# Two MLP boundaries of a three-layer block on one Trainium2 core: the second token tile is normed earlier, GpSimd takes one weight split and one weighting, one square moves between the turned pieces

## The chip, the cores and the metric

One core of a Trainium2 chip runs the whole program: TensorE multiplies, VectorE (DVE in the profile), ScalarE (ACT) and GpSimd (POOL) do the work between the products, and SyncE (SP) issues the loads of the weights. The metric is the device time of one execution in microseconds (us).

## What is computed

Three transformer layers on 512 tokens of width 1024, all in float32. The layers' attention and gating parts don't matter here. What matters is how an MLP ends and what stands behind it:

```
def _rms_norm(x, g):
    y = xf * lax.rsqrt(jnp.mean(xf * xf, axis=-1, keepdims=True) + NORM_EPS)
    return (y * g).astype(x.dtype)

def _squared_relu_mlp(x, w1, w2):
    h = jax.nn.relu(x @ w1)
    return (h * h) @ w2

# layer 0 and layer 1
    f = _squared_relu_mlp(_rms_norm(h, norm_g[layer, 2]), ffn_w1[layer], ffn_w2[layer])
    h = h + _rms_norm(f, norm_g[layer, 3])
# the next part begins with
    xn = _rms_norm(h, norm_g[layer, 0])          # layer 1: the SGU mixer
    h = rms_norm(x, norm_mix[l]) * (1.0 + sc1) + sh1   # third layer: attention
```

So behind each of the two squared-ReLU MLPs a **boundary** follows: square f and weight it with the gain row, add it to h, square h, norm it, turn it (tokens by features to features by tokens), multiply with the next weights. There are two of these boundaries, one behind layer 0 and one behind layer 1.

## The kernel before, in words

**Weights.** All weights pass through two slots `w_raw` of 128x2048. A float32 product is made of three TensorE products of rounded parts: ScalarE writes the rounded part (`split_hi`, L704, `w_hi`), VectorE the rest (`split_lo`, L1347, `w_lo = w_raw - w_hi`), and `mm3` (L2118 to L2120) multiplies hi x hi, hi x lo and lo x hi. SyncE loads tile n as soon as `w_lo_ready` tells that tile n-2 is split.

**Order.** No scheduler: each engine runs one list that is written out by hand, with counting semaphores between them. What stands on an engine behind a waiting instruction waits too.

**A boundary.** Tokens stand in four tiles t of 128 rows; f is in `m` (parts 0 and 1 of the MLP already summed) and in PSUM (the last part). `post` exists once on ScalarE and once on VectorE, with `partial` true at our two boundaries (passes 3 and 7, `p` = 2 and 4). TensorE ends the MLP in `tail`: it finishes the sums of tiles 0, 1, 2, turns tiles 0 and 1 (`transposed`, L2142, 8 transposes each, waits on `xs_ready`, which `normed` of that tile sets), multiplies the last 12 products of tile 3, and then goes into `head`. The head multiplies the first two weight tiles of the next part (`head_hi`, `head_lo`, in places of their own) with tokens 0 to 255 (a = 0), turns tiles 2 and 3, and goes on with tokens 256 to 511 (a = 1). Within the first head tile it waits for each of the eight 128-row pieces of x (`x_ready`).

VectorE's steps in `post` are: `head_split_lo` (L1404: a subtraction of 128x2048 with both inputs in SBUF), `add_sum` (L1463: m + PSUM, 128x1024), `gained` (L1425: m times `row_gain`, both in SBUF), `joined` (L1431: h = m * rstd + h, both in SBUF), `normed` (L1374: h * rstd into m), `turned_lo` (L1396 in the first boundary; L1394, L1390, L1392 in the second, which also adds a bias). ScalarE's are: `head_split_hi` (L801), `sum_square` and `h_square` (L739 with a root, L744; 1024 wide), `turned_hi` (L773; L770, L771, L766 in the second). `rooted` (L1368) is a reciprocal of one column.

**GpSimd** sums the modulation of the third layer in six chunks (`ada_chunk`, L663 tensor_scalar and L664 tensor_tensor of 128x1024, both on SBUF), three of them early in layer 0's MLP and three in layer 1's. Between the halves it masks `w_s` (L675) and makes four small roots, behind them come two iotas. In the boundaries it has nothing but the eight maskings.

Of the kernel before, what the change touches and what calls it, by code (L numbers as in the profile page):

```python
# [20 lines left out]
F32 = mybir.dt.float32  # L21
F32R = mybir.dt.float32r
I32 = mybir.dt.int32
ALU = mybir.AluOpType
# [82 lines left out]
def program(nc, A, out):  # L107

    S, N_TILES, N_UNITS = plan()
# [21 lines left out]
    with ctx:  # L131
# [55 lines left out]
        m = place("m", [P, NT, D], M_)  # L187
# [91 lines left out]
        def sem(name):  # L279
            return ctx.enter_context(nc.semaphore(name))  # L280
# [41 lines left out]
            "h_ready", "gate_used", "y_value", "y_hi_ready", "cmp_loaded", "cmp_x_ready", "cmp_step"))  # L322
        final_done, stored = sem("final_done"), sem("stored")
        tail_gained, tail_rstd = sem("tail_gained"), sem("tail_rstd")

# [50 lines left out]
        def turned_piece(p, a, k):  # L376

            bank_ = 4 * a + (S[HEADS[p]].unit + (0, 1, 0, 1, 2, 3, 2, 3)[k]) % 4
            c = (0, 0, 1, 1, 0, 0, 1, 1)[k] * 256
            return ps[:, bank_, c:c + 256]  # L380
# [218 lines left out]
        def _(pool):  # L599
# [56 lines left out]
            def ada_use(cc, k):  # L656
# [9 lines left out]
                if k == DK - 1:  # L666
                    pool.sem_inc(ada_sum, 1)

            pool.wait_ge(c_ready, 1)
            for cc in range(3):  # L670
                ada_chunk(cc)

            pool.wait_ge(ws_loaded, 16)
# [10 lines left out]
            for cc in range(3, 6):  # L684
                ada_chunk(cc)

            nc.gpsimd.iota(col_no[:, 0:256], pattern=[[1, 256]], base=0, channel_multiplier=0).then_inc(f_made, 1)
# [8 lines left out]
        def _(act):  # L696
# [60 lines left out]

            def turned_hi(p, a):

                for k in range(DK):  # L760
                    src, dst, gain = turned_piece(p, a, k), x_hi[:, k, 256 * a:256 * a + 256], col_gain[:, p, k:k + 1]
                    act.wait_ge(xt_done, x_base(p, a) + (3, 4, 3, 4, 7, 8, 7, 8)[k])
# [18 lines left out]
            def post(pass_no, e, partial, h_before, p):  # L781
# [30 lines left out]
                h_square(1)  # L812
                sum_square(2)
                turned_hi(p, 0)
                sum_square(3)
# [525 lines left out]
        def _(dve):  # L1341
# [76 lines left out]
            def post(pass_no, e, partial, row_no, p):  # L1418
# [23 lines left out]
                joined(1)  # L1442
                normed(0, e + 2)
                if partial:
                    add_sum(pass_no, 2)
                normed(1, e + 3)
                head_split_lo(p, 1)
                turned_lo(p, 0)
                if partial:
                    add_sum(pass_no, 3)  # L1450
                for t in (2, 3):
                    gained(t)
                    joined(t)
                normed(2, e + 6)
# [1494 lines left out]
```

## Time and profile before

| | us |
|---|---|
| median of 3 runs | 2027.57 (2027.54 to 2028.61) |
| the profiled execution | 2027.51 |
| its span | 2025.8 |
| PE busy in the span | 2000.7 (99%) |
| DVE, ACT, POOL busy | 1013.0, 702.0, 340.8 |
| TensorE clock granted | 0.999 |

The span is the part between the first and the last instruction that the profile records; the execution's own time is 1.7 us longer. In the timelines below, the first boundary lies at 640 to 673 us and the second at 1284 to 1318 us. Busy PE says little on its own: what counts is where TensorE stands still, and its idle time is put behind the instruction that ended it.

### The profile page before, as it was taken

The page shows a single profiled execution, that of the slowest core. Times are in us where ns is not written, and L with a number is a line of the kernel's source. Part 1 is how long each engine was busy: PE and PEld are TensorE (multiplying, and loading weights), DVE is VectorE, ACT ScalarE, POOL GpSimd, SP SyncE. Part 2 cuts the span into 40 slices and gives each one's busy share as a digit, 9 for nine tenths or more (in the row PEclk, how much of TensorE's full clock was granted, in tenths as well). Part 3 has the DMA queues.
Part 4 walks back from the last instruction along what each step waited for, and adds up shares of the span by engine and source line. Part 5 has one row for each costly group of instructions (what it writes and reads, how often), then busy time and mean ns, then how long its engine had stood idle before and what let it go on. Part 6 is the DMA issues. An engine that isn't in the chain of part 4 may idle for free.

```text
span 2025.8 us, 26755 instructions
## 1 busy us (share of the span) xinstructions
PE 2000.7 (99%) x10855; PEld 1675.0 (83%) x10855; DVE 1013.0 (50%) x1400; ACT 702.0 (35%) x1012; POOL 340.8 (17%) x199
## 2 busy tenths in 40 slices
PE   9999999999999999999999999999999999999998
PEld 7878888888888888889888888888877788888887
DVE  5358858438255435626735534642443654322345
ACT  6356743232124422315213212533433343212213
POOL 1000006858100001000585720000000200000000
PEclk9999999999999999999999999999999999999999
DMA  6211044544323233132453532222222232332321
GB/s 201 77 49 43 24 133 138 179 130 166 104 95 108 78 104 94 66 111 87 163 187 116 174 112 88 83 84 76 81 64 77 70 104 92 106 104 89 98 104 63
DMA packets 135031, 208.89 MB, mean 103 GB/s; under 512 B 6346, under 2 KB 105864, under 8 KB 134920
## 3 DMA queue, kind: packets, MB, share of 16 engines
q1 hardware_dynamic: 125952, 180.37, 27.5%
q0 software_dynamic: 6912, 25.17, 3.8%
q10 hardware_dynamic: 2056, 1.76, 0.3%
q8 instruction: 84, 1.38, 0.3%
q14 instruction: 27, 0.22, 0.0%
HBM read 205.18 MB, written 2.10 MB: 102 GB/s over the span
## 4 chain that ended last, share of the span: by engine, by line
PE 92%; DVE 4%; ACT 2%; issue 1%; POOL 1%; ACTq 0%; POOLq 0%; DVEq 0%
PE ps L2118 27%; PE ps L2120 27%; PE ps L2119 27%; PE ps L2179 1%; PE ps L2559 1%; PE ps L2570 1%; PE ps L2678 1%; PE ps L2172 1%; PE ps L2171 1%; PE ps L2775 1%; PE ps L2142 1%; POOL gate_t L691 1%; DVE w_lo L1347 0%; ACT w_hi L704 0%; PE ps L2548 0%
## 5 line engine op out<-in xcount | busy, mean ns | idle before, releaser
L1347 DVE TENSOR_TENSOR w_lo<-w_raw,w_hi 128x2048 fp32r<-128x2048 f32 x149 | 347.7, 2334 | 569.5 <-ACT w_hi L704 569.4
L2118 PE MATMUL ps<-x_hi,w_hi 128*128 128x512 f32 x1240 | 489.2, 394 | 1.4 <-ACT v_sw L906 0.8
L2120 PE MATMUL ps<-x_hi,w_lo 128*128 128x512 f32 x1240 | 483.0, 390 | 0.0
L2119 PE MATMUL ps<-x_lo,w_hi 128*128 128x512 f32 x1240 | 482.9, 389 | 0.0
L704 ACT ACTIVATE w_hi<-w_raw 128x2048 fp32r<-128x2048 f32 x151 | 288.9, 1913 | 526.4 <-PE ps L2120 425.4
L2118 PEld LDWEIGHTS ps<-x_hi,w_hi 128*128 128x128 f32 x1240 | 233.2, 188 | 51.9 <-issue 4.6
L2120 PEld LDWEIGHTS ps<-x_hi,w_lo 128*128 128x128 f32 x1240 | 232.7, 188 | 49.0
L2119 PEld LDWEIGHTS ps<-x_lo,w_hi 128*128 128x128 f32 x1240 | 233.0, 188 | 46.2 <-issue 0.2
L2118 PE MATMUL ps<-w_hi,h_hi 128*128 128x512 f32 x688 | 268.2, 390 | 0.0
L2120 PE MATMUL ps<-w_hi,h_lo 128*128 128x512 f32 x688 | 267.7, 389 | 0.0
L2119 PE MATMUL ps<-w_lo,h_hi 128*128 128x512 f32 x688 | 267.7, 389 | 0.0
L2118 PEld LDWEIGHTS ps<-w_hi,h_hi 128*128 128x128 f32 x688 | 129.1, 188 | 27.0 <-issue 0.2
L2119 PEld LDWEIGHTS ps<-w_lo,h_hi 128*128 128x128 f32 x688 | 129.1, 188 | 26.9 <-issue 0.2
L2120 PEld LDWEIGHTS ps<-w_hi,h_lo 128*128 128x128 f32 x688 | 129.1, 188 | 26.9
L663 POOL TENSOR_SCALAR ada_w<-ada_w,cols 128x1024 f32<-128x1024 f32 x42 | 141.5, 3369 | 2.8 <-DMA ada_w<-in_w_ada 0.7
L1090 ACT ACTIVATE work<-ps 128x512 f32<-128x512 f32 x64 | 38.1, 599 | 241.9 <-PE ps L2120 228.2
L664 POOL TENSOR_TENSOR ada_acc<-ada_acc,ada_w 128x1024 f32<-128x1024 f32 x42 | 117.0, 2785 | 3.5
L1741 DVE TENSOR_TENSOR work<-work 128x512 f32<-128x512 f32 x64 | 69.5, 1085 | 94.8 <-ACT work L1090 94.8
L2118 PE MATMUL ps<-w_hi,x_hi 128*128 128x256 f32 (+1 forms) x288 | 96.4, 335 | 0.0
L2119 PE MATMUL ps<-w_lo,x_hi 128*128 128x256 f32 (+1 forms) x288 | 95.0, 330 | 0.0
L2120 PE MATMUL ps<-w_hi,x_lo 128*128 128x256 f32 (+1 forms) x288 | 95.0, 330 | 0.0
L691 POOL TENSOR_TENSOR gate_t<-gate_t 128x512 f32<-128x512 f32 x8 | 12.3, 1580 | 426.8 <-DVE gate_t L2022 426.8
(400 smaller groups left out, 2671.6 us busy)
## 6 DMA issues: line engine op xcount, KB each, us to landing
w_raw<-in_ffn_w SPq DMA_DIRECT2D x64, 1024.0 KB, 5.3
ada_w<-in_w_ada POOLq DMA_DIRECT2D x48, 512.0 KB, 4.2
w_raw<-in_w_ffn_in SPq DMA_DIRECT2D x22, 1024.0 KB, 5.1
w_raw<-in_w_in SPq DMA_DIRECT2D x20, 1024.0 KB, 5.4
w_raw<-in_o_w_in SPq DMA_DIRECT2D x16, 1024.0 KB, 5.5
w_raw<-in_w_ffn_out SPq DMA_DIRECT2D x11, 1024.0 KB, 4.9
w_raw<-in_e_w_in SPq DMA_DIRECT2D x9, 1024.0 KB, 5.3
w_raw<-in_o_w_out SPq DMA_DIRECT2D x8, 1024.0 KB, 4.8
```

The lines of the kernel that those rows point to most:

```text
L663: chain.link(nc.gpsimd.tensor_scalar(ada_w[:, s, :], ada_w[:, s, :], c_col[:, k:k + 1], None, ALU.mult))
L664: add = nc.gpsimd.tensor_tensor(ada_acc[:, cc % 2, :], ada_acc[:, cc % 2, :], ada_w[:, s, :], ALU.add)
L691: nc.gpsimd.tensor_tensor(gate_of(f), gate_of(f), gate_of(DK + f), ALU.add).then_inc(y_value, 1)
L704: nc.scalar.activation(w_hi[:, slot, :], w_raw[:, slot, :], ACT.Copy).then_inc(w_hi_ready, 1)
L1090: nc.scalar.activation(work[:, f, :], ps[:, bank(st, q, f), :], ACT.Relu).then_inc(bank_free, 1)
L1347: nc.vector.tensor_tensor(w_lo[:, slot, :], w_raw[:, slot, :], w_hi[:, slot, :].bitcast(F32), ALU.subtract).then_inc(w_lo_ready, 1)
L1741: chain.link(nc.vector.tensor_tensor(r, r, r, ALU.mult))
L2118: nc.tensor.matmul(dst, a_hi, b_hi, start=start, stop=False)
L2119: nc.tensor.matmul(dst, a_hi, b_lo, start=False, stop=False)
L2120: return nc.tensor.matmul(dst, a_lo, b_hi, start=False, stop=stop_)
L2142: o = nc.tensor.transpose(turned_piece(p, t // 2, k)[:, c:c + P], m[:, t, k * P:(k + 1) * P], ident[:, :])
L2171: nc.tensor.matmul(dst, hi[:, k, blk], x_hi[:, k, toks], start=(k == 0), stop=False)
```

## The change

In `post` with `partial` (only the two boundaries behind the MLPs):

- **VectorE** norms tile 1 before it adds the sum of tile 2, no longer splits the second head tile and no longer weights tile 2; it waits for `third_gained` before `joined(2)`.
- **GpSimd** gets `behind_mlp`: it splits the second head tile once `head_hi` of it is written, and weights tile 2 once the root of tile 2's square is there. The first call stands behind the first three modulation chunks and ahead of the masking of `w_s`, the second behind the last three chunks and ahead of the iotas.
- **ScalarE** squares the sum of tile 2 behind the fourth of the eight turned pieces, no longer ahead of the first.

The other boundaries keep their order. TensorE's and SyncE's lists are unchanged.

```
+            def behind_mlp(p, e, row_no):
+                n = S[HEADS[p]].first + 1
+                pool.wait_ge(w_lo_ready, n)
+                pool.wait_ge(w_hi_ready, n + 1)
+                nc.gpsimd.tensor_tensor(head_lo[p, 1][:, :], w_raw[:, n % 2, :], head_hi[p, 1][:, :].bitcast(F32),
+                                        ALU.subtract).then_inc(w_lo_ready, 1)
+                pool.wait_ge(rows_loaded, 16 * row_no)
+                pool.wait_ge(squares, e + 5)
+                nc.gpsimd.tensor_tensor(m[:, 2, :], m[:, 2, :], row_gain[:, :], ALU.mult).then_inc(third_gained, 1)
...
             for cc in range(3):
                 ada_chunk(cc)
+            behind_mlp(2, 12, 2)
...
             for cc in range(3, 6):
                 ada_chunk(cc)
+            behind_mlp(4, 28, 4)
...
                 for k in range(DK):
+                    if k == 4 and between is not None:
+                        between()
...
-                sum_square(2)
-                turned_hi(p, 0)
+                if partial:
+                    turned_hi(p, 0, lambda: sum_square(2))
+                else:
+                    sum_square(2)
+                    turned_hi(p, 0)
...
                 normed(0, e + 2)
+                normed(1, e + 3)
                 if partial:
                     add_sum(pass_no, 2)
-                normed(1, e + 3)
-                head_split_lo(p, 1)
+                else:
+                    head_split_lo(p, 1)
                 turned_lo(p, 0)
                 if partial:
                     add_sum(pass_no, 3)
-                for t in (2, 3):
-                    gained(t)
-                    joined(t)
+                    dve.wait_ge(third_gained, p // 2)
+                else:
+                    gained(2)
+                joined(2)
+                gained(3)
+                joined(3)
```

VectorE in the second boundary before, from the first norming on:

```order
833 L1374 TENSOR_SCALAR m<-h,rstd 128x1024 [waits dve_chain]
834 L1463 TENSOR_TENSOR m<-m,ps 128x1024 [waits mm_done]
835 L1368 RECIPROCAL rstd<-root 128x1 [waits squares]
836 L1374 TENSOR_SCALAR m<-h,rstd 128x1024 [waits dve_chain]
837 L1404 TENSOR_TENSOR head_lo<-w_raw,head_hi 128x2048 [waits w_hi_ready]
838 L1394 TENSOR_TENSOR x_lo<-work,x_hi 128x256 [waits x_hi_ready]
```

And the same place in the changed kernel:

```order
831 L1392 TENSOR_SCALAR m<-h,rstd 128x1024 [waits dve_chain]
832 L1386 RECIPROCAL rstd<-root 128x1 [waits squares]
833 L1392 TENSOR_SCALAR m<-h,rstd 128x1024 [waits dve_chain]
834 L1485 TENSOR_TENSOR m<-m,ps 128x1024 [waits mm_done]
835 L1412 TENSOR_TENSOR x_lo<-work,x_hi 128x256 [waits x_hi_ready]
```

The second norming stands ahead of the sum of tile 2, and the 128x2048 split is gone from VectorE.

GpSimd in the changed kernel, behind the last modulation chunk (before, L664 and the iota were neighbours):

```order
183 L664 TENSOR_SCALAR ada_w<-ada_w,cols 128x1024 [waits ada_loaded1,pool_chain]
184 L665 TENSOR_TENSOR ada_acc<-ada_acc,ada_w 128x1024 [waits pool_chain]
185 L674 TENSOR_TENSOR head_lo<-w_raw,head_hi 128x2048 [waits pool_chain,w_hi_ready,w_lo_ready]
186 L678 TENSOR_TENSOR m<-m,row_gain 128x1024 [waits squares,rows_loaded]
187 L700 IOTA col_no 128x256
```

The two rows with head_lo and m are new; their inputs are all in SBUF.

ScalarE in the second boundary of the changed kernel, around the fourth piece:

```order
501 L786 ACTIVATE x_hi<-work 128x256 [waits act_chain]
502 L781 ACTIVATE x_hi<-ps,col_bias,cols 128x256 [waits x_ready,xt_done]
503 L752 ACTIVATE ps,ss<-m 128x1024 [waits m_added]
504 L757 ACTIVATE root<-ss,small 128x1 [waits act_chain]
505 L785 ACTIVATE work<-ps,col_bias,cols 128x256 [waits x_ready,xt_done]
```

Before, the square and its root stood ahead of the first piece (rows 497 and 498, ahead of row 499).

## Rows read from the trace of the kernel before

**Rows 1.** Page, busy time of each engine in the span.

```profile
PE 2000.7 (99%) x10855; PEld 1675.0 (83%) x10855; DVE 1013.0 (50%) x1400; ACT 702.0 (35%) x1012; POOL 340.8 (17%) x199
```

**Rows 2.** Timeline of PE, second boundary: start us, us, engine, line, what, [idle before].

```profile
1294.90 1.03 PE L2142 MATMUL ps<-ident,m 128*128 128x128 f32 x8
1297.23 1.09 PE L2142 MATMUL ps<-ident,m 128*128 128x128 f32 x8 [1.30 <-DVE m L1374]
...
1301.43 0.36 PE L2118 MATMUL ps<-x_hi,head_hi 128*128 128x256 f32 x1 [0.35 <-DVE x_lo L1394]
...
1307.26 0.28 PE L2171 MATMUL ps<-x_hi,head_hi 128*128 128x256 f32 x1
...
1312.67 1.09 PE L2142 MATMUL ps<-ident,m 128*128 128x128 f32 x8 [1.42 <-DVE m L1374]
1314.31 1.09 PE L2142 MATMUL ps<-ident,m 128*128 128x128 f32 x8 [0.54 <-DVE m L1374]
```

**Rows 3.** Timeline of PE, first boundary.

```profile
653.49 1.09 PE L2142 MATMUL ps<-ident,m 128*128 128x128 f32 x8 [1.30 <-DVE m L1374]
...
666.94 1.03 PE L2142 MATMUL ps<-ident,m 128*128 128x128 f32 x8
668.36 0.88 PE L2142 MATMUL ps<-ident,m 128*128 128x128 f32 x6 [0.39 <-DVE m L1374]
```

**Rows 4.** Timeline of DVE, second boundary.

```profile
1289.57 1.28 DVE L1431 SCALAR_TENSOR_TENSOR h<-m,rstd,h 128x1024 f32<-128x1024 f32 x1
1291.00 1.23 DVE L1425 TENSOR_TENSOR m<-m,row_gain 128x1024 f32<-128x1024 f32 x1 [0.15 <-ACT root L744]
...
1296.23 0.15 DVE L1368 RECIPROCAL rstd<-root 128x1 f32<-128x1 f32 x1
...
1305.24 1.21 DVE L1463 TENSOR_TENSOR m<-m,ps 128x1024 f32<-128x1024 f32 x1
```

**Rows 5.** Timeline of ACT, second boundary.

```profile
1286.85 1.91 ACT L801 ACTIVATE head_hi<-w_raw 128x2048 fp32r<-128x2048 f32 x1
...
1294.97 0.29 ACT L744 ACTIVATE root<-ss,small 128x1 f32<-128x1 f32 x1
1296.35 1.03 ACT L739 ACTIVATE ps<-m 128x1024 f32<-128x1024 f32 x1 [1.09 <-DVE m L1463]
...
1297.82 0.56 ACT L770 ACTIVATE work<-ps,col_bias,cols 128x256 f32<-128x256 f32 x1
```

**Rows 6.** Timelines of ACT and DVE, same boundary: first and last step of tokens 256 to 511.

```profile
1314.89 0.56 ACT L770 ACTIVATE work<-ps,col_bias,cols 128x256 f32<-128x256 f32 x1 [1.62 <-PE ps L2142]
...
1321.63 0.35 DVE L1392 TENSOR_SCALAR x_lo<-work,col_bias 128x256 fp32r<-128x256 f32 x1
```

**Rows 7.** Lines L664 and L641 of POOL: ns min/median/max, first and last start us.

```profile
L664 POOL TENSOR_TENSOR ada_acc<-ada_acc,ada_w x42: 2384/2414/4231, 327.5 to 1173.9; 128x1024 f32<-128x1024 f32 x42
...
L641 POOL TENSOR_TENSOR o_gla<-o_gla,e_t x4: 1271/1274/1282, 170.7 to 250.4; 128x512 f32<-128x512 f32 x4
```

**Rows 8.** Timelines of ACT and of POOL at the program's start.

```profile
11.92 1.05 ACT L856 ACTIVATE w_hi<-w_raw 128x1024 fp32r<-128x1024 f32 x1
...
13.06 2.57 POOL L627 TENSOR_TENSOR w_lo<-w_raw,w_hi 128x1024 fp32r<-128x1024 f32 x1 [8.40 <-ACT w_hi L856]
```

**Rows 9.** Timelines of DVE and POOL where DVE begins inside POOL's tensor_tensor.

```profile
1154.71 4.48 DVE L1347 TENSOR_TENSOR w_lo<-w_raw,w_hi 128x2048 fp32r<-128x2048 f32 x1 [6.19 <-ACT w_hi L704]
...
1154.65 2.39 POOL L664 TENSOR_TENSOR ada_acc<-ada_acc,ada_w 128x1024 f32<-128x1024 f32 x1
...
495.39 0.16 DVE L1754 TENSOR_TENSOR col_mod<-ps,cols 128x8 f32<-128x8 f32 x1
495.58 2.17 DVE L1760 SCALAR_TENSOR_TENSOR cols<-col_mod,cols 128x8 f32<-128x8 f32 x1
```

**Rows 10.** The same, inside a POOL tensor_scalar.

```profile
1054.94 2.33 DVE L1347 TENSOR_TENSOR w_lo<-w_raw,w_hi 128x2048 fp32r<-128x2048 f32 x1 [7.73 <-ACT w_hi L704]
...
1054.00 2.86 POOL L663 TENSOR_SCALAR ada_w<-ada_w,cols 128x1024 f32<-128x1024 f32 x1
```

More of the change, by code:

```diff
@@ L323, in program @@
         final_done, stored = sem("final_done"), sem("stored")
+        third_gained = sem("third_gained")
         tail_gained, tail_rstd = sem("tail_gained"), sem("tail_rstd")
@@ L756, in first_hi, with turned_hi @@
                     nc.scalar.activation(x_hi[:, k, :], ps[:, k, :], ACT.Copy, scale=col_gain[:, 0, k:k + 1]).then_inc(x_hi_ready, 1)
-            def turned_hi(p, a):
+            def turned_hi(p, a, between=None):
                 for k in range(DK):
+                    if k == 4 and between is not None:
+                        between()
                     src, dst, gain = turned_piece(p, a, k), x_hi[:, k, 256 * a:256 * a + 256], col_gain[:, p, k:k + 1]
```

## The prediction, made before the changed kernel was run

> **What bounds the kernel now.** I read the page's busy times first: TensorE is busy for 2000.7 of 2025.8 us [rows 1], so only its standing still can be won, and whatever makes it stand longer is paid in full. The timelines of PE come second. They show what the two boundaries hold of it: 1.30, 0.35, 1.42 and 0.54 us in the second [rows 2], 1.30 and 0.39 in the first [rows 3]. That is 5.3 us in all, the most that the change could ever give back: 0.26%. Behind the boundaries nothing catches up, since TensorE is the bound, so a shift of the last transposes on which it waits (tile 3's, 668.36 and 1314.31) is a shift of the end. The last steps are what the chain on VectorE and ScalarE between consists of [rows 4, 5], and how VectorE and GpSimd get on where both work on SBUF [rows 9, 10]. That view decides my forecast.
>
> **Part 1: tile 1 normed ahead of the sum of tile 2.** Before, the root of tile 1 was done at 1294.97 + 0.29 = 1295.26 [rows 5], but its reciprocal stood behind the sum and began at 1296.23 [rows 4]. Ahead of it, it begins at about 1295.30: tile 1 comes 0.93 us earlier, in either boundary, and of TensorE's 1.30 us 0.4 stay. The sum of tile 2 moves back by about 1 us; only ScalarE's square of it waits for that, and it has itself been moved behind piece four.
>
> **Part 2: the square of tile 2 in the middle.** From its start at 1296.35 to the first piece at 1297.82 it takes 1.47 us [rows 5]. The first four pieces come earlier, the last four behind it. TensorE goes through the eight pieces of the first head tile in 1301.43 to 1307.26 [rows 2], 48 products of 0.12, three per piece and half of the columns; it takes pieces 1 to 3 for one half of the columns, then for the other, and needs the fifth 2.9 us after it begins. By itself the move costs nothing there, and takes away the 0.35 us at 1301.43.
>
> **Part 3: the split and one weighting go to GpSimd.** VectorE loses about 2.28 and 1.23 us. The split's time mostly filled a wait for ScalarE's pieces. The weighting (L1425, 1.23 [rows 4]) stands in the chain from the sum of tile 3 at 1305.24 to the normings on which TensorE waits at 1312.67 and 1314.31; there some 1.2 us go. If GpSimd's work held nobody, walking the lists through with these durations turns tile 3 in the first boundary 1.3 us earlier (0.93 + 0.39) and in the second 1.1: 2.4 us won, 2025.1. That is the ideal sum, and a rival below.
>
> **GpSimd's price.** It has no subtraction of 128x2048 before. A tensor_tensor of 512 columns takes 1.27 us, of 1024 columns 2.39 undisturbed [rows 7]; 1.12 for each further 512 gives 4.63 for 2048. Twice the 2.57 of the one rounded subtraction of 1024 [rows 8] is 5.14, the upper end. I take 4.63, the fit through two sizes. It starts when ScalarE's second head_hi ends, 1286.85 + 1.91 = 1288.76 [rows 5], plus the 0.09 between the end of L856 at 12.97 and L627 [rows 8].
>
> **What it does to VectorE.** At 1154.71 a VectorE subtraction with both inputs in SBUF began 0.06 us after GpSimd's tensor_tensor. It took 4.48 us, where its line usually takes 2.29: it stood until about 0.14 before GpSimd's end at 1157.04 and then ran in full. At 495.58 a scalar_tensor_tensor of eight columns took 2.17 us, while one that reads PSUM took 0.16 right before it [rows 9]. So a VectorE instruction with two SBUF inputs stands for the rest of a GpSimd tensor_tensor; a sum that reads PSUM doesn't. In the second boundary GpSimd's split would lie at 1288.85 to 1293.48. VectorE's next instruction with two SBUF inputs is joined(0), due at 1289.57 [rows 4]. It can start at 1293.34: **3.77 us late**. Behind it on VectorE is everything that leads to TensorE: gained(1), joined(1), both normings. The first boundary repeats the pattern, 643.74 us earlier (653.49 against 1297.23), with the same 3.77.
>
> The Trainium skill, page "SBUF — State Buffer", section "Who interferes with whom", gives a cause for this: VectorE and GpSimd share a port pair as an exclusive lock that is held for the whole instruction, a VectorE instruction with two SBUF inputs contends with a GpSimd one that reads SBUF, and the issue order decides who is blocked. It speaks against this change. The rows at 1154 and 495 agree [rows 9]. But at 1054.94 a VectorE subtraction that began inside a GpSimd tensor_scalar, which reads SBUF too and ran until 1056.86, took only 2.33 us [rows 10]; by the page it would have been held for 1.9 us more. If the split behaved like that row, the sum would be the 2025.1 above; by the page it is the 2033.4 below. The split is a tensor_tensor, so the rows at 1154 and 495 are the nearest and decide.
>
> **The sum, second boundary.** joined(0) starts at 1293.34, gained(1) at 1294.54 instead of 1291.00, joined(1) at 1296.00, and the first norming ends at 1298.15. TensorE turns tile 0 at 1298.21 instead of 1294.90. Square and root behind joined(1) end at 1298.80, the second norming at 1299.78: tile 1 is turned at 1299.84, 2.61 late, and the head begins at 1303.69. Pieces 1 to 4 are in time. GpSimd's weighting of tile 2 starts with the root of the square in the middle, at about 1305.0, and with 2.39 us holds VectorE off until 1307.26. The remainder of the fifth piece (L1394) has two SBUF inputs and was due at 1306.0: it is done at 1307.68, TensorE wanted it at 1306.57 and stands 1.1 us. Eight pieces take 7.1 us undisturbed, 1.57 for two [rows 6]; with the square and this wait the last is done at 1310.1. So the sum of tile 3 is at 1310.02 instead of 1305.24, joined(2) at 1311.35, gained(3) at 1312.78 behind its root, joined(3) at 1314.23, and the normings end at 1316.37 and 1318.00. Tile 3 is turned at 1318.06 instead of 1314.31: **3.75 us lost**, with the gains of parts 1 to 3 in it.
>
> **The sum, first boundary.** Tile 1 is turned at 656.08 (+2.59). The pieces' remainders read PSUM here, so the weighting blocks nothing, and TensorE reaches the turning of tile 2 at 666.94 + 2.59 = 669.53. VectorE's normings of tiles 2 and 3 end at 668.7 and 670.4, just in time, so the 0.39 us of before go: tile 3 is turned at 670.56 instead of 668.36, **2.20 us lost**. The maskings of w_s, now behind the weighting, are needed only two weight tiles behind the head, and the iotas' reader comes behind the second boundary. SyncE's load behind the split is issued earlier, which nobody waits for.
>
> Together 2.20 + 3.75 = 5.95 us. The profiled execution's own time is 2027.51 (its span and 1.7 us around it), the median 2027.57, so the sum stands on 2027.5: **2033.4 us**, 0.29% slower. Bounds: 5.14 for the split adds 0.5 per boundary: 2034.5. Without the blocked fifth piece the second boundary loses 2.55, not 3.75: 2032.2.
>
> **Rivals.** (a) Faster than before: VectorE isn't held, or only for a moment as under a tensor_scalar [rows 10], and the chain runs as in parts 1 to 3. The time is 2025.1. It decides from the point where joined(0) is held for less than 0.8 us (the fifth piece held too) or 1.2 (not held): then parts 1 to 3 give more than it takes. For it speaks the row at 1054, against it those at 1154 and 495. (b) Half a block: GpSimd lets the port go in the middle of its 2048 columns. joined(0) would be some 1.6 us late, each boundary loses 2.2 less, 2029.1. No row shows it, but none has an instruction this long either. (c) VectorE is first: GpSimd starts over 0.8 us behind its release and has to wait behind joined(0). Then it gets the pause ahead of gained(1) at 1291.00 and holds that off until 1295.3, 0.8 us later than in the sum, in both boundaries: 2035.0. Against it stands the 0.09 [rows 8]. (d) The whole block, a split of 5.14 and the maskings of w_s between VectorE's steps in the first boundary: 2035.
>
> **How the numbers follow.** The forecast (4.7 to 7 us lost: 2032.2 to 2034.5) has 0.72; (a) 0.09; (b) and other partial blocks 0.10; (c) and (d) together 0.09. The likeliest is 2033.4. The range leaves out (a), the lower part of (b) and little above (c) and (d): 2030 to 2035.2. 0.2% is 4.05 us, about what a measurement of this kernel can tell from no change. Slower by more than that (above 2031.6): the forecast, (c), (d) and a little of (b), 0.82. Within: (a) and most of (b), 0.16. Faster by over 0.2% would need 4 of the 5.3 us, where even the ideal sum gives 2.4: 0.02.
>
> **What the changed profile would show.** Part 1 right: the second norming right behind the first on VectorE, the sum of tile 2 behind it. The block right: a GpSimd split of about 4.6 us from 645.1 and 1288.9, in it a joined(0) of about 5 us instead of 1.28, and a wait of some 3 us ahead of tile 0's transposes, where none was. The second block right: the first L1394 behind the square in the middle takes about 1.7 us. What would make the prediction wrong: a joined(0) of 1.3 us inside GpSimd's split (rival a), or a split well over 5 us, which would mean that GpSimd is the one that is held.

## Result: the changed kernel is slower, by about 7.4 us

| | before | after |
|---|---|---|
| median of all runs, us | 2027.57 (7 runs, 2027.39 to 2028.99) | 2034.97 (7 runs, 2033.95 to 2037.17) |
| ratio after to before | | 1.0038, 95% interval 1.0028 to 1.0047 |
| profiled execution: own time, span, us | 2027.51, 2025.8 | 2034.84, 2033.1 |

The direction was forecast, the size not quite: 5.9 us were predicted, the medians differ by 7.4. The forecast gave 4.7 to 7 us lost, 2032.2 to 2034.5, and the median lies above it. The centre of the ratio puts the changed kernel at 2035.3, just above the wide range too, which ended at 2035.2. The seven runs lie apart: four at 2033.95 to 2034.97, three at 2036.48 to 2037.17. The profiled one, 2034.84, is of the four, and what is read from the trace holds for these. So one question is left: which cost of 1.5 us the sum doesn't have.

The page of the changed kernel, busy times, beside [rows 1]:

```profile
PE 2003.5 (99%) x10855; PEld 1678.0 (83%) x10855; DVE 1017.3 (50%) x1396; ACT 701.2 (34%) x1012; POOL 356.7 (18%) x203
```

TensorE has the same 10855 instructions and is busy 2.8 us longer. A longer wait can't do that. This is the first sign of what the sum lacks. VectorE lost four instructions and still is busy 4.3 us longer.

The waits of PE (engine, line waited for, us in total, times, longest), two lines of before and the same two of the changed kernel:

```profile
PE ps L2142 <- DVE m L1374: 5.5, 6, 1.4
...
PE ps L2118 <- DVE x_lo L1394: 0.3, 1, 0.3
```

```profile
PE ps L2164 <- DVE m L1392: 9.3, 6, 3.1
...
PE ps L2140 <- DVE x_lo L1412: 0.9, 1, 0.9
```

So 3.8 us more are waited for the normings and 0.6 more for a remainder: 4.4 us. With the 2.8 us of longer busy time that is 7.2 of the 7.3 us by which the span grew.

**VectorE and GpSimd, changed kernel**, timelines of the two boundaries (start us, us, engine, line). L1449 is joined, L1443 gained, L674 and L678 GpSimd's split and weighting, L1412 a remainder:

```profile
645.71 5.02 DVE L1449 SCALAR_TENSOR_TENSOR h<-m,rstd,h 128x1024 f32<-128x1024 f32 x1
650.65 1.21 DVE L1443 TENSOR_TENSOR m<-m,row_gain 128x1024 f32<-128x1024 f32 x1
...
645.04 4.60 POOL L674 TENSOR_TENSOR head_lo<-w_raw,head_hi 128x2048 fp32r<-128x2048 f32 x1 [131.60 <-ACT head_hi L816]
...
1292.75 5.04 DVE L1449 SCALAR_TENSOR_TENSOR h<-m,rstd,h 128x1024 f32<-128x1024 f32 x1
...
1306.62 0.42 DVE L1412 TENSOR_TENSOR x_lo<-work,x_hi 128x256 fp32r<-128x256 f32 x1 [0.24 <-ACT x_hi L786]
1309.34 1.87 DVE L1412 TENSOR_TENSOR x_lo<-work,x_hi 128x256 fp32r<-128x256 f32 x1 [1.40 <-ACT x_hi L786]
...
1292.08 4.62 POOL L674 TENSOR_TENSOR head_lo<-w_raw,head_hi 128x2048 fp32r<-128x2048 f32 x1 [113.35 <-ACT head_hi L816]
1308.55 2.39 POOL L678 TENSOR_TENSOR m<-m,row_gain 128x1024 f32<-128x1024 f32 x1 [11.84 <-ACT root L757]
```

Read the first and the third row together. GpSimd's split starts at 645.04 and lasts 4.60 us. VectorE's joined(0) begins 0.67 us inside it and lasts 5.02 us where it took 1.28 [rows 4]: it stood for 3.74 us, until 649.45, and GpSimd ended at 649.64. At 1309.34 the remainder behind the square takes 1.87 instead of 0.42 us, inside the weighting.

**TensorE, changed kernel**: five rows of the first boundary, then the second boundary from tile 0 on:

```profile
654.30 1.09 PE L2164 MATMUL ps<-ident,m 128*128 128x128 f32 x8 [3.11 <-DVE m L1392]
655.93 1.97 PE L2164 MATMUL ps<-ident,m 128*128 128x128 f32 x8 [0.54 <-DVE m L1392]
657.55 0.78 PE L2140 MATMUL ps<-w_hi,h_hi 128*128 128x512 f32 x1
658.12 0.63 PE L2141 MATMUL ps<-w_lo,h_hi 128*128 128x512 f32 x1
...
670.69 1.91 PE L2164 MATMUL ps<-ident,m 128*128 128x128 f32 x16
...
1301.36 3.34 PE L2164 MATMUL ps<-ident,m 128*128 128x128 f32 x16 [3.12 <-DVE m L1392]
...
1311.27 0.38 PE L2140 MATMUL ps<-x_hi,head_hi 128*128 128x256 f32 x1 [0.95 <-DVE x_lo L1412]
...
1320.03 1.09 PE L2164 MATMUL ps<-ident,m 128*128 128x128 f32 x8 [1.48 <-DVE m L1392]
1321.66 1.09 PE L2164 MATMUL ps<-ident,m 128*128 128x128 f32 x8 [0.54 <-DVE m L1392]
```

The wait of 3.1 us ahead of tile 0 is the forecast one. Behind it is something that no row of before shows at a boundary: the eight transposes of tile 1 take 1.97 instead of 1.09 us and the first products 0.78 and 0.63 instead of 0.39. The view by stretches has the granted clock (length, PE, PEld, DVE, ACT and POOL busy, then the clock as a share of full speed, the DMA share, GB/s):

```profile
655.00:657.00 2.00, 1.46 (x9) 1.22 (x8) 1.97 (x3) 0.13 (x1) 0.00 (x0) 0.67 0.00 0
657.00:660.00 3.00, 3.00 (x13) 2.54 (x12) 1.76 (x5) 2.72 (x7) 0.00 (x0) 0.65 0.00 0
1298.00:1302.00 4.00, 0.88 (x5) 0.65 (x4) 3.21 (x6) 2.71 (x6) 0.00 (x0) 0.85 0.81 257
1302.00:1304.00 2.00, 2.00 (x12) 1.94 (x11) 1.97 (x3) 0.00 (x0) 0.00 (x0) 0.50 0.00 0
```

0.50 is the lower of the clock's two levels, 1.2 GHz; 0.67 is a stretch that lies partly in it. Cut finer, the clock reads 0.50 from 656.0 to 659.0 and from 1301.0 to 1304.0, so in the second boundary it fell while TensorE was still standing. In the kernel before all stretches of both boundaries read 1.00.

**Where the time went, by boundary.** TensorE does the same work behind each boundary in every kernel, so the start of the same product, compared with before, is the time lost so far. I use the first product with w and x behind the first boundary's head (682.72 before) and the first product of the layer behind the second's (1328.66). What a run was early or late ahead of the first boundary is taken off.

| kernel | first, us lost | second, us lost | median of runs |
|---|---|---|---|
| predicted | 2.20 | 3.75 | 2033.4 |
| after | 3.27 | 4.21 | 2034.97 |
| late split | -1.57 | 4.69 | 2029.10 |
| without GpSimd | 1.53 | 2.43 | 2031.45 |
| one input | 1.74 | 4.34 | 2033.34 |
| eight pieces | 0.03 | 1.94 | 2029.50 |
| weighting back | 3.55 | 3.64 | 2034.89 |
| 22 products | 2.84 | 6.06 | 2034.96 |
| 14 products | 2.03 | 5.25 (3.72 at tile 3) | 2033.36 |
| late split, first boundary only | -1.58 | 0.02 | 2027.31 |

The boundaries are read from the one profiled execution, the medians are of all. The rows behind the second are the experiments below.

These losses hold falls of the clock too. It reads 0.50 for about 3 us, besides both boundaries of the changed kernel, in both of one input and of weighting back, and in the second alone of without GpSimd (from 1316.5), eight pieces (from 1298.5), 22 and 14 products (from 1321.5) and, twice, late split (from 1303.0 and 1316.5). The late split in the first boundary only has none. So the second column doesn't give the price of the hold by itself.

### The profile page after: what moved, and what is told of

Same layout as the page of the kernel before. It is cut to its first block, busy times and chain, and to the rows that moved or that the text cites. A ratio compares the mean times of both kernels' runs of the same rounds, so it can differ in the third digit from the quotient of the medians.

```text
span 2033.1 us, 26759 instructions
## 1 busy us (share of the span) xinstructions
PE 2003.5 (99%) x10855; PEld 1678.0 (83%) x10855; DVE 1017.3 (50%) x1396; ACT 701.2 (34%) x1012; POOL 356.7 (18%) x203
## 4 chain that ended last, share of the span: by engine, by line
PE 92%; DVE 4%; ACT 2%; issue 1%; POOL 1%; ACTq 0%; POOLq 0%; DVEq 0%
PE ps L2140 27%; PE ps L2142 27%; PE ps L2141 27%; PE ps L2201 1%; PE ps L2581 1%; PE ps L2164 1%; PE ps L2194 1%; PE ps L2193 1%; PE ps L2592 1%; PE ps L2700 1%; PE ps L2797 1%; POOL gate_t L704 1%; DVE w_lo L1365 0%; ACT w_hi L717 0%; PE ps L2570 0%
## 5 line engine op out<-in xcount | busy, mean ns | idle before, releaser
L664 POOL TENSOR_SCALAR ada_w<-ada_w,cols 128x1024 f32<-128x1024 f32 x42 | 143.0, 3406 | 2.8 <-DMA ada_w<-in_w_ada 0.6
L651 POOL DMA_DIRECT2D ada_w<-in_w_ada x48 | 28.6, 595 | 319.6 <-DVE h_lo L1748 195.2
```

What stands on the lines that cost most here:

```text
L651: pool.dma_start(ada_w[:, s, :], A["w_ada_2"][0, k * P:(k + 1) * P, cc * 1024:(cc + 1) * 1024])\
L664: chain.link(nc.gpsimd.tensor_scalar(ada_w[:, s, :], ada_w[:, s, :], c_col[:, k:k + 1], None, ALU.mult))
```

## The experiments

Ratios are to the kernel before, whose median in the three sets of runs was 2027.55 to 2027.59 us.

### The hold, taken away: a split that starts later

```diff
                 pool.wait_ge(w_hi_ready, n + 1)
+                pool.wait_ge(xs_ready, 4 * p + 2)
                 nc.gpsimd.tensor_tensor(head_lo[p, 1][:, :], ...
```

> The changed kernel, but GpSimd's split of the second head tile waits until tile 1 is normed. Theory (VectorE is held by GpSimd's tensor_tensor if it has two SBUF inputs): joined(0) is back at 1.28 us in both boundaries. First boundary: the pieces' remainders read PSUM and are not held, tile 3 is turned 1.3 us earlier than in the kernel before. Second boundary: the first remainder (L1412) is held for 2.9 us, the one behind the square again; 3 to 4 us lost. Together 2029 to 2031 us. Rival (what costs is not the hold but that the split is on the slower engine, or the new order): 2035 or more, as the split is ready later still.

Measured: 2029.10 us (2028.87 to 2030.94, 11 runs), ratio 1.0010 (1.0001 to 1.0019): 5.9 us less than the changed kernel. joined(0) takes 1.28 us in both boundaries. The first boundary now gains 1.6 us against before. The second loses 4.7 in the profiled execution, where 3 to 4 were expected for both effects. The split has only moved there, onto the first remainder, for which TensorE waits 2.85 us, and the clock falls twice behind that and the next wait. This execution (own time 2030.78) is of the upper of two groups of runs, 2028.9 to 2029.1 and 2030.5 to 2030.9. DVE, then POOL:

```profile
1296.51 3.35 DVE L1413 TENSOR_TENSOR x_lo<-work,x_hi 128x256 fp32r<-128x256 f32 x1 [0.55 <-ACT x_hi L787]
...
1295.00 4.58 POOL L675 TENSOR_TENSOR head_lo<-w_raw,head_hi 128x2048 fp32r<-128x2048 f32 x1 [120.86 <-DVE m L1393]
```

So the hold of joined(0) and what follows from it are the main cost. In the first boundary its removal is worth 3.27 + 1.57 = 4.8 us: about 3.7 of the hold and, as the run with 14 products below shows, 1.2 of the clock. What decides is what VectorE has to do beside the 4.6 us: in the first boundary remainders that read PSUM, in the second ones with both inputs in SBUF.

### GpSimd left out: the new orders alone

```diff
-            behind_mlp(2, 12, 2)
...
-            behind_mlp(4, 28, 4)
...
-                else:
-                    head_split_lo(p, 1)
+                head_split_lo(p, 1)
...
-                    dve.wait_ge(third_gained, p // 2)
-                else:
-                    gained(2)
+                gained(2)
```

> Only the new orders: tile 1 normed ahead of the sum of tile 2, the square in the middle of the pieces; both the split and the weighting of tile 2 stay on VectorE, GpSimd gets nothing. Theory (most of the loss is GpSimd's hold): joined(0) takes 1.28 us, no wait of 3 us ahead of tile 0; but the last four pieces come 1.5 us later behind the square, and nothing shortens the chain behind them: 1.9 us lost in the first boundary, 1.2 in the second, 2030.6 us. Rival (the new orders cost what the changed kernel lost): 2035.

Measured: 2031.45 us (2030.22 to 2031.98, 11 runs), ratio 1.0016 (1.0007 to 1.0025). Parts 1 and 2 by themselves lose time too: TensorE's wait ahead of tile 1 falls from 1.30 to 0.37 us as forecast, but VectorE's split, now behind the sum of tile 2, delays the pieces' remainders, and TensorE waits 1.5 us for x_lo and up to 2.5 for a norming. The first boundary loses 1.5 us, the second 2.4, where 1.9 and 1.2 were expected; the clock fell in the second, behind the wait of 2.5 us. The new order needs the split to be elsewhere. It doesn't by itself cost what the changed kernel lost: with split and weighting on VectorE it costs 3.9 us, with both on GpSimd 7.4.

### How long VectorE is held: one input, and eight pieces

```diff
-                nc.gpsimd.tensor_tensor(head_lo[p, 1][:, :], w_raw[:, n % 2, :], head_hi[p, 1][:, :].bitcast(F32),
-                                        ALU.subtract).then_inc(w_lo_ready, 1)
+                nc.gpsimd.tensor_scalar(head_lo[p, 1][:, :], w_raw[:, n % 2, :], 0.0, None,
+                                        ALU.mult).then_inc(w_lo_ready, 1)
```

> The changed kernel, but GpSimd's split is a tensor_scalar with one SBUF input (w_raw times 0) of the same size: it leaves out the remainder part of the second head tile's weights in both boundaries. GpSimd's instruction takes about 5.6 us (2.85 per 1024 columns). Theory from the rows of before (VectorE is held only for about the first 1 us of a tensor_scalar of 1024 columns): joined(0), due 0.7 us behind its start, takes 1.6 to 2.6 us, the time is 2026.5 to 2028.5. Rival (held for the whole GpSimd instruction that reads SBUF, whatever its inputs): joined(0) takes 6.0 us, 2037.

Measured: 2033.34 us (2032.78 to 2034.66, 6 runs), ratio 1.0028 (1.0016 to 1.0040). Timelines of DVE and POOL:

```profile
645.68 4.07 DVE L1449 SCALAR_TENSOR_TENSOR h<-m,rstd,h 128x1024 f32<-128x1024 f32 x1
...
645.04 5.38 POOL L674 TENSOR_SCALAR head_lo<-w_raw 128x2048 fp32r<-128x2048 f32 x1 [133.21 <-ACT head_hi L816]
```

Neither expectation held. joined(0) stood for 2.79 us, until 648.47: 3.4 us into an instruction of 5.38, and 1.95 us before its end. The second boundary has the same (4.07, inside 5.37). With a GpSimd instruction of one input VectorE is let go earlier, but by no means at once. The time is no measure of the hold here, since the clock fell in both boundaries, behind waits of 2.15 and 1.46 us. The row at 1054.94 [rows 10], 0.94 us into a tensor_scalar of half the width, wasn't held. Other rows of before tell when such a one lets go, this pair of DVE and POOL for one:

```profile
1165.59 3.02 DVE L1347 TENSOR_TENSOR w_lo<-w_raw,w_hi 128x2048 fp32r<-128x2048 f32 x1 [6.40 <-ACT w_hi L704]
...
1165.34 2.86 POOL L663 TENSOR_SCALAR ada_w<-ada_w,cols 128x1024 f32<-128x1024 f32 x1
```

VectorE's split takes 2.29 us elsewhere, so it stood for 0.73 us, until 1166.32: 0.98 us into the tensor_scalar and 1.88 before its end. At 354.16 and 983.95 it is the same within 0.05 us. So at 1024 and at 2048 columns VectorE was let go some 1.9 us ahead of the recorded end, and not a fixed time or share behind the start. The expectation had taken the 1 us from the start to hold for the longer one too. What ends at that moment in GpSimd no run here shows.

The other run cuts the split into eight:

```diff
-                nc.gpsimd.tensor_tensor(head_lo[p, 1][:, :], w_raw[:, n % 2, :], head_hi[p, 1][:, :].bitcast(F32),
-                                        ALU.subtract).then_inc(w_lo_ready, 1)
+                for c in range(0, TILE, 256):
+                    part = slice(c, c + 256)
+                    o = nc.gpsimd.tensor_tensor(head_lo[p, 1][:, part], w_raw[:, n % 2, part],
+                                                head_hi[p, 1][:, part].bitcast(F32), ALU.subtract)
+                o.then_inc(w_lo_ready, 1)
```

> The changed kernel with GpSimd's split cut into eight tensor_tensor of 256 columns. By the prices of 512 and 1024 columns (1.27 and 2.39 us, 1.12 for 512 more) one takes about 0.71 us, all of them 5.7. Theory A (VectorE is held until the GpSimd instruction that is running ends, and gets its turn between two): joined(0) takes at most 1.28 + 0.7 us, the three or four VectorE instructions with two SBUF inputs that lie beside the split are late by 0.35 us each on the mean, tile 0 is turned 1 to 2 us late instead of 3.3, and the time is 2029 to 2031.5. Theory B (a queue of ready GpSimd instructions keeps VectorE off until the last is done): joined(0) takes over 6 us and the time is 2036 to 2037.

Measured: 2029.50 us (2029.09 to 2030.76, 10 runs), ratio 1.0010 (1.0000 to 1.0019). VectorE's steps beside it, and the range of the pieces (ns min/median/max):

```profile
646.00 1.85 DVE L1452 SCALAR_TENSOR_TENSOR h<-m,rstd,h 128x1024 f32<-128x1024 f32 x1
647.77 1.76 DVE L1446 TENSOR_TENSOR m<-m,row_gain 128x1024 f32<-128x1024 f32 x1
649.76 1.45 DVE L1452 SCALAR_TENSOR_TENSOR h<-m,rstd,h 128x1024 f32<-128x1024 f32 x1
...
651.32 1.04 DVE L1395 TENSOR_SCALAR m<-h,rstd 128x1024 f32<-128x1024 f32 x1
...
652.96 1.23 DVE L1395 TENSOR_SCALAR m<-h,rstd 128x1024 f32<-128x1024 f32 x1
...
L676 POOL TENSOR_TENSOR head_lo<-w_raw,head_hi x16: 720/1172/1723, 645.3 to 1297.4; 128x256 fp32r<-128x256 f32 x16
```

Now they take turns. VectorE's steps with two SBUF inputs are late by 0.57, 0.53 and 0.17 us. The two normings have one such input and still take 1.04 and 1.23 us instead of 0.75, so it isn't only two-input steps that wait. The remainders that read PSUM keep their 0.88 us for two beside a GpSimd split (at 653.79 in the late split's trace). And GpSimd waits too: its undisturbed piece of 0.72 us (0.71 estimated) has a median of 1.17, and the eight take 9.43 us instead of 5.8. TensorE's waits ahead of tiles 0 and 1 are 0.93 and 0.73 us instead of 3.11 and 0.54, and the first boundary loses nothing. In the second, behind the same two waits of 0.93 and 0.73 us, the clock fell, and 1.9 us are lost:

```profile
1298.00:1302.00 4.00, 4.00 (x15) 3.52 (x16) 2.91 (x6) 3.06 (x7) 0.53 (x1) 0.57 0.58 158
```

Theory A holds: the hold ends with the running instruction, not with the queue.

### The weighting, given back to VectorE

```diff
-                pool.wait_ge(rows_loaded, 16 * row_no)
-                pool.wait_ge(squares, e + 5)
-                nc.gpsimd.tensor_tensor(m[:, 2, :], m[:, 2, :], row_gain[:, :], ALU.mult).then_inc(third_gained, 1)
...
-                    dve.wait_ge(third_gained, p // 2)
-                else:
-                    gained(2)
+                gained(2)
```

> The changed kernel with the weighting of tile 2 back on VectorE, behind the sum of tile 3; the split stays on GpSimd. Theory A (the two effects that the prediction gave the weighting cancel): in the second boundary the first remainder behind the square takes 0.8 instead of 1.87 us and TensorE's 0.95 us ahead of it go, but 1.23 us stand again in VectorE's chain to the normings of tiles 2 and 3; in the first boundary the same 1.23 us turn TensorE's arrival at tile 2 just in time into a wait of 0 to 1 us. 2034.8 to 2036. Theory B (GpSimd's weighting is a net cost, its hold of the remainder worth more than the step it takes off VectorE): 2033.8.

Measured: 2034.89 us (2034.42 to 2036.00, 5 runs), ratio 1.0036 (1.0023 to 1.0050): the same as the changed kernel. The parts are seen in the trace. The remainder behind the square takes 0.42 us and TensorE's 0.95 ahead of it are gone, and the wait ahead of tile 2 has grown from 1.48 to 1.90. The second boundary loses 3.6 instead of 4.2 us, the first 3.55 instead of 3.27. Two things are mixed into this. GpSimd's maskings now follow the split at once, beside gained(1), which takes 1.30 instead of 1.21 us, so that tile 0 is waited for 3.29 us in the first boundary; and the clock fell in both boundaries as in the changed kernel. With that said, the two effects cancel within what the median can tell, as theory A said.

### TensorE kept busy while it waits

```diff
+                if p in (2, 4) and t == 0:
+                    pe.wait_ge(squares, {2: 12, 4: 28}[p] + 1)
+                    for _ in range(22):
+                        nc.tensor.matmul(ps[:, 0, 0:P], ones[:, :], ident[:, :], start=True, stop=True)
                 pe.wait_ge(xs_ready, 4 * p + t + 1)
```

> The changed kernel with 22 dummy products of TensorE (128x128, into a bank that tile 0's transposes overwrite) ahead of tile 0's transposes in both boundaries; they fill about 2.6 of the 3.1 us in which TensorE stands. Theory: the changed kernel loses 5.95 us by the held joined(0) and about 1.5 us more because TensorE's granted clock falls to its lower level behind that standstill (0.67 and 0.65 in the stretches at 655 to 660 us of its trace). Then here the clock stays at 1.00 in both boundaries, joined(0) still takes 5.0 us, and the time is 2033.5 us, 1.5 below the changed kernel. Rival: the 1.5 us are not of the clock: the time stays at 2035.0.

Measured: 2034.96 us (2034.69 to 2036.11, 5 runs), ratio 1.0036 (1.0022 to 1.0049). This looks like a refutation of the clock. The trace says that the experiment was badly sized: the 22 products took 4.9 us, from 650.94 to 655.85, where TensorE had only 3.1 to wait. Tile 0 was turned 1.6 us later than in the changed kernel, and of what the clock gave back little was left: the first boundary loses 2.84 instead of 3.27 us, with the clock at 1.00. In addition the profiled execution, the slowest of the five, had the clock fall at another place, behind the wait of 1.5 us ahead of tile 2 in the second boundary (0.92 from 1318 to 1322, 0.54 from 1322 to 1325). So I ran it again with as many products as fit:

```diff
-                    for _ in range(22):
+                    for _ in range(14):
```

> The changed kernel with 14 products of ones and identity (0.22 us each, 3.1 us) ahead of tile 0's transposes in both boundaries: as long as TensorE stands there (3.11 and 3.12 us), and not 4.9 us as the 22 of the run before. Theory A (the third cost is TensorE's granted clock, which falls to its lower level behind the 3.1 us of standing): the clock reads 1.00 from 655 to 660 and from 1298 to 1307, the first products behind the transposes take 0.39 and not 0.78 us, the first boundary loses 2.2 to 2.4 instead of 3.27 us, the second 3.8 instead of 4.2, and the time is 2033.3 to 2033.7. Theory B (the clock costs nothing, since VectorE's chain is late anyway): 2034.9, as the changed kernel. If the clock falls instead at tile 2's wait of 1.5 us in the second boundary, as in the profiled execution with 22 products, some 1.5 us come back in those executions.

Measured: 2033.36 us (2033.22 to 2035.89, 8 runs, six of them within 2033.22 to 2033.42), ratio 1.0029 (1.0019 to 1.0040). Timeline of PE in the first boundary (this execution runs 1.25 us later than that of the changed kernel from before the boundary on), and three stretches. The trace counts two instructions for each of the 14 products:

```profile
652.28 3.29 PE L2164 MATMUL ps<-ident,ones 128*128 128x128 f32 x28
655.56 1.09 PE L2168 MATMUL ps<-ident,m 128*128 128x128 f32 x8
657.20 1.09 PE L2168 MATMUL ps<-ident,m 128*128 128x128 f32 x8 [0.54 <-DVE m L1392]
658.04 0.48 PE L2140 MATMUL ps<-w_hi,h_hi 128*128 128x512 f32 x1
658.36 0.39 PE L2141 MATMUL ps<-w_lo,h_hi 128*128 128x512 f32 x1
...
670.48 2.14 PE L2168 MATMUL ps<-ident,m 128*128 128x128 f32 x16
```

```profile
655.00:657.00 2.00, 1.65 (x14) 1.23 (x12) 1.28 (x3) 1.12 (x3) 0.00 (x0) 1.00 0.37 137
657.00:660.00 3.00, 2.81 (x17) 2.46 (x18) 2.77 (x6) 1.97 (x5) 0.00 (x0) 1.00 0.00 0
...
1302.00:1304.00 2.00, 1.46 (x13) 1.22 (x12) 1.97 (x3) 0.46 (x1) 0.00 (x0) 1.00 0.00 0
```

By the medians the products that compute nothing make the kernel 1.6 us faster. The intervals of the two ratios overlap, but six of the eight runs are shorter than the shortest of the changed kernel (2033.95), and the trace shows where it comes from. VectorE's chain is the same (joined(0) 5.04 us), the tiles are turned at the same points of it, and only what TensorE does behind is quicker: tile 1's transposes 1.09 instead of 1.97 us, the first products 0.48 and 0.39 instead of 0.78 and 0.63. The first boundary loses 2.03 us instead of 3.27. In the second, tile 3 is turned at 1321.19; less the 3.16 us by which this execution was late ahead of that boundary, 1318.03. The forecast was 1318.06. The profiled execution is again one in which the clock fell behind tile 2's wait, which cost it 1.5 us there; that is why it took 2035.89.

### A version faster than both

The first boundary gained 1.6 us with the late split, the second has no place for it. So: the first as changed with the late split, the second as before.

```diff
 def behind_mlp(p, e, row_no):
...
+                pool.wait_ge(xs_ready, 4 * p + 2)
...
             behind_mlp(2, 12, 2)
...
-            behind_mlp(4, 28, 4)
```

with the orders of ScalarE and VectorE switched by p == 2 in the same way.

> The first boundary as changed, with the split on GpSimd only from tile 1's norming on; the second boundary as before the change. Theory A (the new order with a split that holds nobody wins what the prediction's parts 1 to 3 say, and it comes through to the end): in the first boundary 1.3 to 1.4 us less standing (1.30 and 0.39 become 0.3 and 0), the second as before with 1.30, 0.35, 1.42 and 0.54; 2026.2, beside 2027.6 before. Theory B (the gain in the first boundary is given back in the weight tiles behind it): 2027.6.

Measured: 2027.31 us (2025.78 to 2027.88, 11 runs), ratio 0.9996 (0.9987 to 1.0005). A median of no use, since the runs fall into two groups: five at 2025.8 to 2026.1, six at 2027.3 to 2027.9. The profiled one is of the first group. Its first boundary has only this standing of TensorE left, beside 1.30 and 0.39 us before:

```profile
651.31 1.03 PE L2167 MATMUL ps<-ident,m 128*128 128x128 f32 x8
652.71 1.09 PE L2167 MATMUL ps<-ident,m 128*128 128x128 f32 x8 [0.37 <-DVE m L1392]
```

The middles of the two groups lie 1.7 us apart, near the 1.5 that a fall of the clock had cost in the run with 14 products. So the last two kernels fill TensorE's waits of 1.30 and 1.42 us in the second boundary with products, one on top of this kernel, one on top of the kernel before:

```diff
+                if p == 4 and t in (1, 2):
+                    for _ in range(4 + t):
+                        nc.tensor.matmul(turned_piece(p, t // 2, 0)[:, (t % 2) * P:(t % 2) * P + P],
+                                         ones[:, :], ident[:, :], start=True, stop=True)
                 pe.wait_ge(xs_ready, 4 * p + t + 1)
```

> The kernel with the changed first boundary and the late split, and in its second boundary (as before the change) five products of ones and identity ahead of tile 1's transposes and six ahead of tile 2's, 0.22 us each, so that TensorE works through its waits of 1.30 and 1.42 us. Theory A (that kernel's executions of 2027.3 to 2027.9, six of eleven beside five of 2025.8 to 2026.1, are those in which the granted clock falls behind one of these waits): all or nearly all executions come to 2025.8 to 2026.2, 1.4 us under the kernel before. Theory B (the spread comes from elsewhere): executions at 2027.3 to 2027.9 stay, about as many as before.

Measured: 2025.92 us (2025.79 to 2027.06, 11 runs, ten of them within 2025.79 to 2026.01), ratio 0.9990 (0.9981 to 1.0000). By the medians that is 1.7 us less than before, and the longest of the eleven is shorter than the shortest of the 21 of before (2027.31). By the medians it beats both kernels, by 0.08% and 0.44%; the interval of its ratio to the kernel before just reaches 1, so the gain of 0.08% rests on how closely the runs lie.

> The kernel before with the same eleven products in its second boundary. Theory A: its executions of 2028.6 to 2029.3 (4 of 26 so far) vanish and the others stay at 2027.3 to 2027.9. Theory B: one in six stays there. Both give a median of 2027.5, so this one tells how the products themselves cost (nothing expected), and what the late split's kernel is to be compared with.

Measured: 2027.55 us (2027.45 to 2028.33, 11 runs), ratio 0.9998 (0.9989 to 1.0007), beside 2027.58 of the kernel before, six of whose 21 runs in this set lay between 2028.66 and 2029.52. None of the eleven is that long (the longest is 2028.33), and the products themselves cost nothing:

```profile
1294.13 1.28 PE L2166 MATMUL ps<-ident,ones 128*128 128x128 f32 x10
1295.60 1.09 PE L2171 MATMUL ps<-ident,m 128*128 128x128 f32 x8 [0.19 <-DVE m L1392]
...
1309.46 1.50 PE L2166 MATMUL ps<-ident,ones 128*128 128x128 f32 x12
1311.05 1.09 PE L2171 MATMUL ps<-ident,m 128*128 128x128 f32 x8
```

These rows are of the faster kernel, timeline of PE in its second boundary. In both kernels the longer executions all but go when TensorE works through its waits, as theory A says. No longer execution of either was traced, so that it is the clock which falls in them is inferred from the run with 14 products, not seen.

## Where the prediction was right, and the step that failed

| step | predicted | measured |
|---|---|---|
| GpSimd's split | 4.63 us | 4.60, 4.62 |
| joined(0) late by | 3.77 us, both boundaries | 3.74, 3.76 |
| remainder behind the square | 1.7 us | 1.87 |
| TensorE stands for it | 1.1 us | 0.95 |
| GpSimd's weighting | 2.39 us | 2.41, 2.39 |
| TensorE turns tile 2, first boundary | 669.53 | 670.81; 669.36 at full clock |
| first boundary | 2.20 us lost | 3.27; 2.03 at full clock |
| second boundary, tile 3 | 3.75 us lost | 4.20; 3.72 at full clock |

The times of tile 2 are those of the traces, less what the execution was early or late ahead of the first boundary (0.12 early, 1.12 late). "At full clock" is the run with 14 products.

**Part 1** was right: the second norming stands right behind the first and the sum of tile 2 behind it (the run without GpSimd shows the wait of 1.30 us at 0.37). **Part 2** was right as to TensorE's wait for the fifth piece. **Part 3** was right to 0.03 us in the hold and in the length of the split. The page "SBUF — State Buffer" of the Trainium skill, section "Who interferes with whom", says that the lock is held for the whole instruction. For the tensor_tensor the trace agrees: joined(0) was released 0.2 us before GpSimd's end. For the tensor_scalar it doesn't: joined(0) was released 1.95 us before its end.

**The step that failed is TensorE's own pace behind its standing: "TensorE reaches the turning of tile 2 at 666.94 + 2.59 = 669.53", was worked out with the durations of before, and so was the second boundary from "TensorE turns tile 0 at 1298.21" on. What the stand costs the products behind it was put at nothing, without a reason.** TensorE did turn tile 0 as forecast: 1301.36, less the 3.15 us by which it was late ahead of the second boundary, is 1298.21. But its granted clock fell to 1.2 GHz at the 3.1 us of standing, the products that followed took up to twice as long, and tile 2 of the first boundary was turned at 670.81, 1.28 us later than forecast. With the wait filled it was 669.36. By the difference between the changed kernel and the one with 14 products that is 3.27 - 2.03 = 1.24 us in the first boundary and 4.20 - 3.72 = 0.48 in the second, together 1.7; the medians say 2034.97 - 2033.36 = 1.6. (Of the shorter group of each, four runs and six, the means differ by 1.2. TensorE's busy time grew by more, 2.8 us, probably since part of the longer work lies in time in which it would have waited later.) In the second boundary VectorE's chain is what TensorE waits for next, and hides most of it; in the first nothing does, because there TensorE reached tile 2 later than VectorE's norming. The sum 2.20 + 3.75 was right for a TensorE at full clock, and with it the time is 2033.36 us, as predicted to 0.1. The parts were off by 0.17 and 0.03 us, so a little of that closeness is luck.

**Of the rivals**, (a) was wrong by its condition: joined(0) was held for 3.74 us, not under 0.8. Its ideal sum, though, is half shown: where the split holds nobody the first boundary gains 1.6 us, 1.3 were predicted. (b), half a block, isn't seen with a tensor_tensor. The tensor_scalar lets go before its end, but joined(0) stood 2.79 us for it, not 1.6. (c) did not occur, GpSimd was first in both boundaries. (d), the maskings in between, did not cost: they began at 662.69, joined(2) at 663.78 took its usual 1.28 us beside them, and TensorE had no wait at tiles 2 and 3 of the first boundary. The range was too narrow on its upper side since all its bounds were of VectorE and GpSimd: none allowed the bounding engine a change of its own pace.

What stays open: in which executions the clock falls behind waits under 2 us. At the wait of 1.46 to 1.48 us ahead of tile 2 in the second boundary it fell in four traces (late split, one input, 22 and 14 products) and not in two (changed kernel, eight pieces); with eight pieces it fell behind 0.93 and 0.73 us in one boundary and not behind the same two in the other. The one traced execution of before has none, while 6 of 23, 4 of 26 and 6 of 21 runs of the three sets lie where such a fall would put them, above 2028.5; with the first boundary changed it was 6 of 11. With the waits filled it is none of 11 and, of the other kernel, one of 11 off the group. That filling the waits makes such runs rare is shown, what chooses them isn't. The three runs of the changed kernel above 2036.4 weren't traced either; a second fall is likely, not shown. Nor is it shown that the ideal gain of 1.1 us in the second boundary can be had.

## To carry to other kernels

Before work is given to an idle GpSimd, list what VectorE does during it: a GpSimd tensor_tensor stopped each VectorE instruction with two SBUF inputs read here until about its end, so place it beside VectorE work that reads PSUM, or cut it into pieces and accept that both take turns (2029.50 instead of 2034.97 us here, still slower than before). A wait of the bounding engine costs more than its length if the engine's clock falls behind it: compare its busy time with the same instruction count, and look at the granted clock of the stretches behind each new wait. Where TensorE must wait anyway, products of no use that fill the wait exactly are a cheap remedy; 1.6 us too many gave nothing back here.

## What the runs showed of the hardware

- TensorE's granted clock read 0.50 at or behind its waits of 3.1 us, in both boundaries of the changed kernel and of the one with the weighting back, and 1.00 there when 14 products filled the wait. It fell in four of six traces behind a wait of 1.5 us too, which cost about 1.5 us in the run with 14 products, and once behind two waits of 0.93 and 0.73 us.
- VectorE was released 0.2 us before the end of GpSimd's tensor_tensor of 4.6 us, but 1.95 us before the end of a tensor_scalar of 5.38 us and 1.88 us before the end of one of 2.86 us. Beside eight short tensor_tensor its one-input tensor_scalar took 1.04 and 1.23 us instead of 0.75.
- Eight GpSimd instructions of 0.72 us each took 9.43 us beside VectorE's work instead of 5.8, while VectorE's two-input steps were late by 0.2 to 0.6 us each: the hold works both ways.
